# The second mixer of a two-layer trunk: the z tile between q and k, a weight residual behind the z scaling, turned output tiles in four PSUM banks, and the last two of them amid the early rows

## The chip, the cores and the metric

The kernel runs on one core of one Trainium2 chip. The metric is the device time of one execution in microseconds (us). Engines are named as in the profile: PE is TensorE (PEld its weight loads), DVE VectorE, ACT ScalarE, POOL GpSimd, SP the queue that issues most DMAs.

## The reference, cut to what matters

Two layers on 512 tokens of 1024 features, fp32. Layer 0 has a softmax mixer with forget gates and layer 1 a gated linear attention (GLA); each is followed by a squared-ReLU MLP of 4096. The change touches only the GLA mixer:

```python
def gla_mixer(h, w_in, w_gate_up, b_gate, g_norm, w_out):
    proj = h @ w_in                       # q 512, k 512, v 1024, z_lr 16, r 1024 columns
    q, k, v, z_lr, r = split(proj)
    g = log_sigmoid(z_lr @ w_gate_up + b_gate) / 16.0
    # 4 heads of 128 keys and 256 values, causal, decayed by exp(cumsum(g));
    # a state is carried from chunk to chunk
    o = o * rsqrt(mean(o * o) + EPS) * g_norm * silu(r)
    return o @ w_out
```

## The kernel before

**Precision.** Every fp32 weight unit (128 x 2048) and every activation is split into a high part that PE takes in its fast fp32r form (`w_hi`, `hT_hi`, made by ACT) and the residual (`w_lo`, `hT_lo`, made by DVE from the high part and the source). A product is three matmuls: lo·hi, hi·hi, hi·lo. `split_lo(0, 0, c)` makes the residual of weight unit c on DVE; `w_lo_made` counts the units in order. Four slots hold the units; SP loads unit c when `w_lo_made` says that unit c-4 is split.

**Order.** Each engine runs one instruction list that is written out by hand; semaphores carry the dependencies. An instruction that waits holds back all that stands behind it on its engine. There are eight PSUM banks of 128 x 512 fp32.

**Start of the GLA mixer.** PE projects q of head 0 (`project_gqk(0, 0)`, bank 0) and k of head 0 (`project_gqk(0, 1)`, bank 1), 24 matmuls of 512 columns each. Then four blocks against a matrix of ones put the norm's factor into bank 2 (L1492), which ACT copies out as `rstd_wide` (L871). Then comes the z tile (`gate_tile(3, 1)`, L1050 and L1054, 16 matmuls into bank 3). DVE scales it into `zT` (L1894) after the residuals of units GLA_U+1 to GLA_U+3 (`GR_U[0]` is GLA_U+3, the r weights of head 0). Then come the four gate tiles (L1498, two instructions each, banks 4 to 7). ACT and DVE turn these into the log-decays `gb`; v, r and the attention of head 0 follow.

**Attention of a head.** `level(a, lv)` is one of eight score products (L1424) into banks 0 and 1 in turn; DVE prepares its operands (`differences`, `decayed`) and merges its result (`keep`), ACT takes the exponentials (`decays`). `turn_tail(a)` transposes decayed keys through bank 2, `outer(a)` forms the state updates in banks 2 and 3, and `attend(a)` writes the outputs there (L1451, then L1455, which wait for the last `keep`). `project_gr(a, t)` projects r of head a, token block t, into banks 4 and 5; ACT's `tanhs` (L899) and DVE's `silus` (L1967, two instructions a head, counted by `silu_made`) turn it into silu(r).

**Turned output.** `turn_go(k)` transposes feature tile k of the mixer's output (four PE transposes, L1471). ACT's `keep_goT` (L910) makes its high part from that bank, and DVE's `keep_goT` (L1993) the residual, counted by `goT_lo_made`. Tiles 0 to 5 (heads 0 to 2) are turned amid the levels of head 3, by turns in banks 6 and 7. Tiles 6 and 7 need head 3's own output. The output projection starts early: `out_early(0, t)` takes feature tiles 0 to 3 and `out_early(1, t)` tiles 4 and 5 of token block t (L1034, L1037, L1038), and `add_rows` adds tiles 6 and 7, then the second half of the columns.

The two passages of PE's list that are reordered stand in the diff below. ACT's list near the second one is: `decays(3, 4)`, `tanhs(3, (0, 1))`, `decays(3, 5)`, `tanhs(3, (2, 3))`, `keep_goT(0)`, `keep_goT(1)`, `decays(3, 6)`, `keep_goT(2)`, `keep_goT(3)`, `turn_tail(3)`, `keep_goT(4)`, `keep_goT(5)`, `decays(3, 7)`. DVE's is: `keep(3, 2)`, `differences(3, 5)`, `decayed(3, 4)`, `silus(3)`, `differences(3, 6)`, `keep_goT(0)`, `keep_goT(1)`, `keep(3, 3)`, `decayed(3, 5)`, `keep_goT(2)`, `keep_goT(3)`, `keep(3, 4)` and on.

Of the kernel before, what the change touches and what calls it, by code (L numbers as in the profile page):

```python
# [17 lines left out]
TB = S // P  # L18
D = 1024
KT = D // P  # L20
# [6 lines left out]
GLA_H = 4  # L27
# [53 lines left out]
OUT_EARLY = 6  # L81
# [15 lines left out]


def goT_bank(k):
    return 6 + k % 2 if k < OUT_EARLY else k % 2  # L100


def turn_banks(head):
# [68 lines left out]
def fox_gla_trunk(nc, x, fox_w_in, fox_b_f, fox_w_out, gla_w_in, gla_w_gate_up, gla_b_gate,  # L172
# [12 lines left out]
    with ExitStack() as ctx:  # L185
# [829 lines left out]
        def _(pe):  # L1015
# [31 lines left out]
            def gate_tile(b, which, before):  # L1047

                def hi_and_lo(k):
                    return pe.matmul(bank[b][0:GATE_ROWS, :], gates_split[:, k, which * RANK:which * RANK + GATE_ROWS],  # L1050
                                     hT_hi[:, k, :], start=(k == 0), stop=(k == KT - 1))

                def hi_only(k):
                    pe.matmul(bank[b][0:RANK, :], gates_split[:, k, which * RANK:(which + 1) * RANK], hT_lo[:, k, :],  # L1054
                              start=False, stop=False)

                before(0)
                hi_and_lo(0)
                for k in range(1, KT):
                    before(k)  # L1060
                    hi_only(k - 1)
                    if k < KT - 1:
                        hi_and_lo(k)
                hi_only(KT - 1)
                a = hi_and_lo(KT - 1)
                return a
# [65 lines left out]
            def add_rows(i, per, c, x, ready_rows, early=False, between=None, done=0):  # L1132


                for half in range(2):
                    for kg in range(2):
                        j = 2 * half + kg
                        split_of(i, per, c + j)
                        if half == 0:
                            ready_rows(kg)  # L1140
                        for t in range(TB):
                            w, ks = unit(i, per, c + j), range(4 * kg, 4 * kg + 4)
                            if done and half == 0:
                                if kg == 0:
                                    continue
                                w, ks = [b[:, done - KT // 2:] for b in w], range(done, KT)
                            a = block_of_tokens(bank[sum_bank(half, t, early)][:], t, w, x, ks,
                                                kg == 0, kg == 1, t == 0)
                            if kg == 1:
                                a.then_inc(sum_done, 1)  # L1150
                        if between and j == 2:
                            between()
# [208 lines left out]
            def project_gqk(a, part, ks, before=None):  # L1361

                first = QK_BANK[0] if a == 0 else QK_BANK[1]
                w = [x[:, :, part * DK:(part + 1) * DK] for x in unit(0, 0, GQK_U[a], 2 * DK)]
                if (before or ks[0] == 0) and part == 0:
                    split_of(0, 0, GQK_U[a])
                    if a == 1:
                        pe.wait_ge(gv_copied, TB)
                    elif a:
                        pe.wait_ge(gk_copied, a)  # L1370
                to = bank[first + part][:]
                for k in ks:
                    if before:
                        before(k)
                    mm = pe.matmul(to, w[0][:, k, :], hT_lo[:, k, :], start=(k == (ks[0] if before else 0)), stop=False)  # L1375
                    if k == (ks[0] if before else 0) and part == 0:
                        mm.then_inc(w_begun, 1)
                    pe.matmul(to, w[0][:, k, :], hT_hi[:, k, :], start=False, stop=False)
                    mm = pe.matmul(to, w[1][:, k, :], hT_hi[:, k, :], start=False, stop=(k == (ks[-1] if before else KT - 1)))
                if before or ks[-1] == KT - 1:  # L1380
                    mm.then_inc((gq_done, gk_done)[part], 1)
# [18 lines left out]
            def project_gr(a, t):  # L1400

                if t == 0:
                    split_of(0, 0, GR_U[a])
                    pe.wait_ge(gv_copied, 2 if a < 2 else 2 * TB)
                    if a:
                        pe.wait_ge(silu_made, a * 2)
                mm = block_of_tokens(bank[4 + t // 2][:, (t % 2) * DV:(t % 2 + 1) * DV], t, unit(0, 0, GR_U[a], DV), hT,
                                     range(KT), True, True, t == 0)
                if t % 2:
                    mm.then_inc(r_done, 1)  # L1410

            def level(a, lv):

                if lv:
                    pe.wait_ge(ql_made, a * (2 * LEVELS) + 2 * lv)
                    qs, ks = ql[:, lv % 2, :], kl[:, lv % 2, :]
                else:
                    pe.wait_ge(gk_copied, a + 1)
                    pe.wait_ge(gq_copied, a + 1)
                    qs, ks = gq, gk  # L1420
                if a * (LEVELS + 1) + lv > 1:
                    pe.wait_ge(level_kept, a * (LEVELS + 1) + (lv - 1))
                for t in range(TB):
                    mm = pe.matmul(bank[LEVEL_BANK[lv % 2]][:, t * P:(t + 1) * P], ks[:, t * P:(t + 1) * P],  # L1424
                                   qs[:, t * P:(t + 1) * P], start=True, stop=True)
                mm.then_inc(level_done, 1)
# [33 lines left out]
            def turn_go(k):  # L1460
                if k < OUT_EARLY:
                    if k < 2:
                        pe.wait_ge(gk_copied, GLA_H)
                        pe.wait_ge(go_made, 3 * TB)
                    else:
                        pe.wait_ge(goT_lo_made, k - 1)
                else:
                    pe.wait_ge(go_made, GLA_H * TB)
                    pe.wait_ge(level_kept, GLA_H * (LEVELS + 1))
                for t in range(TB):  # L1470
                    mm = pe.transpose(bank[goT_bank(k)][:, t * P:(t + 1) * P], o_all[:, t, k * P:(k + 1) * P], ident[:])  # L1471
                mm.then_inc(go_turned, 1)
# [12 lines left out]

            lo, hi = range(KT // 2), range(KT // 2, KT)
            project_gqk(0, 0, ORDER[2], ready_late(2, GLA_ADDS))
            project_gqk(0, 1, range(KT))
            pe.wait_ge(gla_filled, 2)
            pe.wait_ge(only_made, 1)  # L1490
            for t in range(TB):
                mm = pe.matmul(bank[2][:, t * P:(t + 1) * P], root[:], only[:, t, :], start=True, stop=True)  # L1492
            mm.then_inc(wide_done, 1)
            gate_tile(3, 1, lambda k: None).then_inc(z_done, 1)
            pe.wait_ge(gup_loaded, 48)
            pe.wait_ge(z_scaled, 1)
            for a in range(GLA_H):
# [79 lines left out]
            level(3, 1)  # L1577
            project_gr(3, 2)
            level(3, 2)
            project_gr(3, 3)  # L1580
            turn_go(0)
            turn_go(1)
            level(3, 3)
            turn_go(2)
            turn_go(3)
# [10 lines left out]
            out_early(0, 2)  # L1596
            attend(3)
            out_early(0, 3)
            for t in range(TB):
                out_early(1, t)  # L1600
            turn_go(6)
            turn_go(7)
            add_rows(0, 0, GLA_OUT_U, hT, lambda kg: pe.wait_ge(goT_lo_made, 4 * kg + 4), False,
                     lambda: turn_left(3, MLP1_ADDS), OUT_EARLY)
            turn_right(3, MLP1_ADDS)
# [4 lines left out]
        def _(dve):  # L1610
            mine = Steps(dve, dve_step)

            def split_lo(i, per, c):

                slot = slot_of(c)
                dve.wait_ge(w_hi_made, i * per + (c + 1))
                dve.tensor_tensor(w_lo[:, slot, :], w_stage[:, slot, :], fp(w_hi[:, slot, :]),
                                  ALU.subtract).then_inc(w_lo_made, 1)
# [201 lines left out]
            def keep_qk(h):  # L1820
                dve.wait_ge(qk_hi_made, h + 1)
                dve.scalar_tensor_tensor(out=qk_lo[:], in0=bank[qk_bank(h)][:], scalar=qk_scale[:, 0:1], in1=fp(qk_hi[:]),
                                         op0=ALU.mult, op1=ALU.subtract).then_inc(qk_lo_made, 1)
# [62 lines left out]
            mlp(0, MLP0_U, MLP0_ADDS)  # L1886


            for unit in range(GLA_U + 1, GR_U[0] + 1):
                split_lo(0, 0, unit)  # L1890
            dve.wait_ge(z_done, 1)
            dve.wait_ge(gla_filled, 3)
# [18 lines left out]
            def gates(a):  # L1911

                dve.wait_ge(g_min, a + 1)
                dve.wait_ge(g_ln, min(a, 1) + 1)
                mine.then(dve.tensor_tensor(gb[:, a, :], gb[:, a, :], glog[:, a, :], ALU.subtract))
                dve.wait_ge(gla_filled, 4)
                dve.tensor_tensor_scan(gb[:, a, :], flat(restart[:]), gb[:, a, :], 0.0, ALU.mult, ALU.add).then_inc(gb_made, 1)
# [79 lines left out]
            for a in range(GLA_H):  # L1997
                dve.wait_ge(g_abs, a + 1)
                dve.tensor_scalar(gb[:, a, :], bank[4 + a][:], 0.0, None, ALU.min).then_inc(g_min, 1)
            keep_qk(0)  # L2000
            gates(0)
            differences(0, 1)
            tail_differences(0)
# [164 lines left out]
```

## Time and profile before

| what | value |
|---|---|
| time, median of 3 runs | 1178.92 us (1178.91, 1178.92 and 1181.81) |
| the profiled execution's own time | 1183.01 us |
| its span, first to last instruction | 1181.2 us |
| PE busy | 1157.6 us, 98% of the span |
| mean granted PE clock | 0.994 of full speed |
| GLA mixer, from q of head 0 to the last output sum | about 595 to 846 us |

A row of a timeline is a start in us, a duration in us, the engine and line, the operation with output and inputs and, behind x, how many instructions were merged. In brackets stands the engine's idle time before it and what ended it. A matmul's shown duration has its drain in it, so neighbouring matmuls overlap: the step from start to start is what one costs. A 512-column matmul steps by about 0.23 us, a 256-column one by 0.12 us, and a 128-column one or a transpose by 0.11 us.

### The profile page before, as it was taken

The numbers are of one execution on the slowest core, as the hardware profiler recorded it, in microseconds if no ns is written. First come the engines' busy times: TensorE is split into PE (matmuls) and PEld (weight loads), VectorE is DVE, ScalarE is ACT, GpSimd is POOL, SyncE is SP. The second block draws the span as 40 slices with busy tenths as digits, with TensorE's granted clock in tenths as the row PEclk, the third lists the DMA queues.
The fourth block names the chain that finished last, engine by engine and source line by source line (L and its number), as shares of the span: only waits on it lengthen the run. The fifth ranks groups of instructions, "written<-read, shape, count | busy, mean of one in ns | idle before, by whom it ended". The sixth has DMA issues, their size and how long they took to land.

```text
span 1181.2 us, 14703 instructions
## 1 busy us (share of the span) xinstructions
PE 1157.6 (98%) x5629; PEld 967.2 (82%) x5629; DVE 792.8 (67%) x986; ACT 558.9 (47%) x780; POOL 42.3 (4%) x90
## 2 busy tenths in 40 slices
PE   6999999999999999999999999999999999999997
PEld 5788888888888888888868998987888888888886
DVE  5537778635875856858856585493378578488487
ACT  6336666527434435435555332252455354363454
POOL 2000000000000000000020101010000000000001
PEclk9999999999999999999999999999999999999999
DMA  9248565432062161241540320204132513415202
GB/s 285 51 91 167 126 144 152 129 113 82 26 208 77 48 201 36 86 163 36 162 126 1 108 79 30 72 1 143 36 107 65 185 36 106 144 36 178 74 36 86
DMA packets 116136, 119.00 MB, mean 101 GB/s; under 512 B 38929, under 2 KB 84017, under 8 KB 116082
## 3 DMA queue, kind: packets, MB, share of 16 engines
q1 hardware_dynamic: 112992, 116.21, 32.9%
q10 hardware_dynamic: 3090, 2.05, 0.6%
q8 instruction: 36, 0.59, 0.2%
q14 instruction: 18, 0.15, 0.0%
HBM read 103.50 MB, written 2.10 MB: 89 GB/s over the span
## 4 chain that ended last, share of the span: by engine, by line
PE 95%; DVE 2%; ACT 1%; DMA 1%; issue 1%; POOL 0%; SPq 0%; POOLq 0%; ACTq 0%; DVEq 0%
PE bank L1025 10%; PE bank L1021 10%; PE bank L1024 10%; PE bank L1179 9%; PE bank L1184 8%; PE bank L1183 8%; PE bank L1034 6%; PE bank L1037 6%; PE bank L1038 6%; PE bank L1254 2%; PE bank L1258 2%; PE bank L1257 2%; PE bank L1424 2%; PE bank L1302 2%; PE bank L1289 1%; PE bank L1375 1%
## 5 line engine op out<-in xcount | busy, mean ns | idle before, releaser
L1626 DVE TENSOR_TENSOR w_lo<-w_stage,w_hi 128x2048 fp32r<-128x2048 f32 x88 | 200.5, 2286 | 33.4 <-ACT w_hi L628 11.9
L628 ACT ACTIVATE w_hi<-w_stage 128x2048 fp32r<-128x2048 f32 x80 | 152.0, 1912 | 148.9 <-PE bank L1179 92.4
L1021 PE MATMUL bank<-hT_lo,w_hi 128*128 128x512 f32 x512 | 199.8, 390 | 0.0
L1025 PE MATMUL bank<-hT_hi,w_lo 128*128 128x512 f32 x512 | 199.3, 389 | 0.0
L1024 PE MATMUL bank<-hT_hi,w_hi 128*128 128x512 f32 x512 | 199.2, 389 | 0.0
L1179 PE MATMUL bank<-w_lo,u_hi 128*128 128x512 f32 x336 | 131.7, 392 | 0.0
L1184 PE MATMUL bank<-w_hi,u_lo 128*128 128x512 f32 x336 | 130.8, 389 | 0.0
L1183 PE MATMUL bank<-w_hi,u_hi 128*128 128x512 f32 x336 | 130.8, 389 | 0.0
L1034 PE MATMUL bank<-w_lo,hT_hi 128*128 128x512 f32 (+1 forms) x320 | 116.5, 364 | 4.3 <-DVE hT_lo L1993 1.9
L1021 PEld LDWEIGHTS bank<-hT_lo,w_hi 128*128 128x128 f32 x512 | 96.1, 188 | 20.6 <-DVE hT_lo L1684 0.5
L1037 PE MATMUL bank<-w_hi,hT_hi 128*128 128x512 f32 (+1 forms) x320 | 112.4, 351 | 0.0
L1025 PEld LDWEIGHTS bank<-hT_hi,w_lo 128*128 128x128 f32 x512 | 96.1, 188 | 19.9
L1024 PEld LDWEIGHTS bank<-hT_hi,w_hi 128*128 128x128 f32 x512 | 96.1, 188 | 19.7
L1038 PE MATMUL bank<-w_hi,hT_lo 128*128 128x512 f32 (+1 forms) x320 | 112.3, 351 | 0.0
L1732 DVE SCALAR_TENSOR_TENSOR h<-bank,columns_of,h 128x512 f32<-128x512 f32 x112 | 80.6, 743 | 32.9 <-PE bank L1184 32.9
L715 ACT ACTIVATE u_raw<-bank 128x512 f32<-128x512 f32 x64 | 37.7, 590 | 90.2 <-PE bank L1025 90.0
L1179 PEld LDWEIGHTS bank<-w_lo,u_hi 128*128 128x128 f32 x336 | 63.1, 188 | 15.2 <-DVE h L1732 1.4
L1640 DVE TENSOR_TENSOR w_stage<-w_stage 128x2048 f32<-128x2048 f32 x32 | 73.2, 2286 | 1.2
L1184 PEld LDWEIGHTS bank<-w_hi,u_lo 128*128 128x128 f32 x336 | 63.1, 188 | 13.1
L1183 PEld LDWEIGHTS bank<-w_hi,u_hi 128*128 128x128 f32 x336 | 63.1, 188 | 12.9
L1034 PEld LDWEIGHTS bank<-w_lo,hT_hi 128*128 128x128 f32 x320 | 61.4, 192 | 13.5 <-issue 3.6
L1037 PEld LDWEIGHTS bank<-w_hi,hT_hi 128*128 128x128 f32 x320 | 61.6, 193 | 7.9 <-issue 0.5
(226 smaller groups left out, 1957.4 us busy)
## 6 DMA issues: line engine op xcount, KB each, us to landing
w_stage<-in_mlp_w_up_dram SPq DMA_DIRECT2D x32, 1024.0 KB, 5.6
w_stage<-in_mlp_w_down_dram SPq DMA_DIRECT2D x32, 1024.0 KB, 6.3
w_stage<-in_fox_w_in_dram SPq DMA_DIRECT2D x32, 256.0 KB, 4.7
w_stage<-in_gla_w_in_dram SPq DMA_DIRECT2D x8, 1024.0 KB, 5.3
w_stage<-in_fox_w_in_dram SPq DMA_DIRECT2D x4, 1024.0 KB, 8.7
qa<-qk_hi SPq DMA_DIRECT2D x32, 128.0 KB
w_stage<-in_fox_w_out_dram SPq DMA_DIRECT2D x4, 1024.0 KB, 5.4
w_stage<-in_gla_w_in_dram SPq DMA_DIRECT2D x8, 512.0 KB, 5.1
```

The costliest lines, as they stand in the source:

```text
L628: act.activation(w_hi[:, HI_SLOT[unit], :], w_stage[:, STAGE[unit], :], ACT.Copy).then_inc(w_hi_made, 1)
L1021: a = pe.matmul(out, w[0][:, k, :], x[1][:, k, :], start=(k == 0), stop=False)
L1024: pe.matmul(out, w[0][:, k, :], x[0][:, k, :], start=False, stop=False)
L1025: a = pe.matmul(out, w[1][:, k, :], x[0][:, k, :], start=False, stop=(k == KT - 1))
L1034: a = pe.matmul(out, xs[0], w[1][:, m, :], start=(first and m == 0), stop=False)
L1037: pe.matmul(out, xs[0], w[0][:, m, :], start=False, stop=False)
L1038: a = pe.matmul(out, xs[1], w[0][:, m, :], start=False, stop=(last and m == len(ks) - 1))
L1179: a = pe.matmul(out, xs[0], lo[:, k, :], start=(begins and k == 0), stop=False, skip_group_check=True)
L1183: pe.matmul(out, xs[0], hi[:, k, :], start=False, stop=False, skip_group_check=True)
L1184: a = pe.matmul(out, xs[1], hi[:, k, :], start=False, stop=(k == KT // 2 - 1), skip_group_check=True)
L1626: dve.tensor_tensor(w_lo[:, to, :], w_stage[:, at, :], fp(w_hi[:, to, :]), ALU.subtract).then_inc(w_lo_made, 1)
L1732: dve.scalar_tensor_tensor(out=to, in0=bank[PRODUCTS[n][2] + t][:], scalar=scale, in1=to, op0=ALU.mult, op1=ALU.add).then_inc(added, 1)
```

## The change

`gate_tile` moves from behind k and the ones product to the place between q and k of head 0, and the ones product goes between the two halves of k. On DVE the residual of unit GLA_U+3 moves from ahead of the scaling of z to behind the scaling of q and k of head 0. `goT_bank` puts tiles 2 and 3 in banks 4 and 5, so that the first four turned tiles have four banks; these two wait for the two `silus` of head 3, and tiles 4 and 5 now for tiles 0 and 1. `project_gr(3, 3)` moves behind `turn_go(0)` and `turn_go(1)`, and `turn_go(6)` and `turn_go(7)` move two rows forward in the second early pass. The arithmetic and the number of instructions stay as they were.

```diff
 def goT_bank(k):
-    return 6 + k % 2 if k < OUT_EARLY else k % 2
+    return 2 + k if k in (2, 3) else 6 + k % 2 if k < OUT_EARLY else k % 2
...
                     if k < 2:
                         pe.wait_ge(gk_copied, GLA_H)
                         pe.wait_ge(go_made, 3 * TB)
+                    elif k < 4:
+                        pe.wait_ge(silu_made, 2 * GLA_H + k - 3)
                     else:
-                        pe.wait_ge(goT_lo_made, k - 1)
+                        pe.wait_ge(goT_lo_made, k - 3)
...
             project_gqk(0, 0, ORDER[2], ready_late(2, GLA_ADDS))
-            project_gqk(0, 1, range(KT))
+            gate_tile(3, 1, lambda k: None).then_inc(z_done, 1)
+            project_gqk(0, 1, lo)
             pe.wait_ge(gla_filled, 2)
             pe.wait_ge(only_made, 1)
             for t in range(TB):
                 mm = pe.matmul(bank[2][:, t * P:(t + 1) * P], root[:], only[:, t, :], start=True, stop=True)
             mm.then_inc(wide_done, 1)
-            gate_tile(3, 1, lambda k: None).then_inc(z_done, 1)
+            project_gqk(0, 1, hi)
             pe.wait_ge(gup_loaded, 48)
             pe.wait_ge(z_scaled, 1)
...
             level(3, 1)
             project_gr(3, 2)
             level(3, 2)
-            project_gr(3, 3)
             turn_go(0)
             turn_go(1)
+            project_gr(3, 3)
             level(3, 3)
             turn_go(2)
             turn_go(3)
...
             attend(3)
             out_early(0, 3)
-            for t in range(TB):
+            for t in range(2):
                 out_early(1, t)
             turn_go(6)
             turn_go(7)
+            for t in range(2, TB):
+                out_early(1, t)
             add_rows(0, 0, GLA_OUT_U, hT, lambda kg: pe.wait_ge(goT_lo_made, 4 * kg + 4), False,
...
-            for unit in range(GLA_U + 1, GR_U[0] + 1):
+            for unit in range(GLA_U + 1, GR_U[0]):
                 split_lo(0, 0, unit)
             dve.wait_ge(z_done, 1)
...
             keep_qk(0)
+            split_lo(0, 0, GR_U[0])
             gates(0)
```

## Rows read from the trace of the kernel before

**Rows 1.** The page, its span and PE's busy time.
```profile
span 1181.2 us, 14703 instructions
PE 1157.6 (98%) x5629; PEld 967.2 (82%) x5629; DVE 792.8 (67%) x986; ACT 558.9 (47%) x780; POOL 42.3 (4%) x90
```
**Rows 2.** Waits of PE: who waited for whom, total us, times, longest us.
```profile
PE bank L1034 <- DVE hT_lo L1993: 1.9, 1, 1.9
...
PE bank L1471 <- DVE hT_lo L1993: 1.6, 1, 1.6
PE bank L1498 <- DVE zT L1894: 0.9, 1, 0.9
```
**Rows 3.** Windows of 5 us: busy of PE, PEld, DVE, ACT, POOL; PE clock; DMA.
```profile
615.00:620.00 5.00, 5.00 (x11) 2.88 (x10) 3.23 (x6) 3.16 (x5) 0.00 (x0) 0.50 0.61 214
620.00:625.00 5.00, 5.00 (x20) 4.05 (x19) 3.96 (x8) 4.93 (x6) 0.00 (x0) 0.83 0.00 0
...
780.00:785.00 5.00, 3.42 (x31) 3.23 (x30) 4.84 (x12) 3.14 (x6) 0.00 (x0) 1.00 0.00 0
...
815.00:820.00 5.00, 5.00 (x16) 3.92 (x17) 2.29 (x1) 0.68 (x1) 0.00 (x0) 0.66 0.15 29
820.00:825.00 5.00, 5.00 (x23) 4.12 (x22) 0.51 (x1) 1.92 (x1) 0.00 (x0) 1.00 1.03 363
```
**Rows 4.** Timeline of all engines around the z tile and the gate tiles.
```profile
607.05 1.05 PE L1492 MATMUL bank<-only,root 128*128 128x128 f32 x8
...
608.14 0.60 ACT L871 ACTIVATE o_all<-bank 128x512 f32<-128x512 f32 x1 [0.67 <-PE bank L1492]
...
609.11 2.28 DVE L1617 TENSOR_TENSOR w_lo<-w_stage,w_hi 128x2048 fp32r<-128x2048 f32 x1
...
611.83 0.68 DVE L1894 TENSOR_TENSOR zT<-bank,o_all 48x512 f32<-48x512 f32 x1 [0.45 <-PE bank L1050]
...
612.66 4.94 PE L1498 MATMUL bank<-zT,gup 65*128 65x512 f32 x8 [0.87 <-DVE zT L1894]
...
633.27 0.42 DVE L1935 TENSOR_TENSOR ql<-gq,decay 128x256 f32<-128x256 f32 x1 [8.45 <-ACT decay L890]
```
**Rows 5.** Timeline of PE, ACT and DVE, levels 2 to 5 of head 3.
```profile
777.52 1.06 PE L1424 MATMUL bank<-ql,kl 128*128 128x128 f32 x8
...
781.29 1.03 PE L1471 MATMUL bank<-ident,o_all 128*128 128x128 f32 x8
...
781.87 0.82 ACT L899 ACTIVATE gb<-bank,half_rstd 128x256 f32<-128x256 f32 x2
...
782.72 0.69 DVE L1967 SCALAR_TENSOR_TENSOR gb<-gb,bank 128x512 f32<-128x512 f32 x1 [0.16 <-ACT gb L899]
...
784.80 1.31 PE L1471 MATMUL bank<-ident,o_all 128*128 128x128 f32 x8 [1.58 <-DVE hT_lo L1993]
...
785.95 0.41 DVE L1935 TENSOR_TENSOR ql<-gq,decay 128x256 f32<-128x256 f32 x1
...
788.56 1.06 PE L1424 MATMUL bank<-ql,kl 128*128 128x128 f32 x8
```
**Rows 6.** Timeline, end of head 3's attention: its last merge, and PE at `attend`.
```profile
799.06 0.73 DVE L1950 COPY_PREDICATED o_all<-masks,bank 128x512 f32<-128x512 uint8 x1
...
800.76 1.46 PE L1451 MATMUL bank<-state,since 128*128 128x256 f32 x6
...
802.06 1.89 PE L1455 MATMUL bank<-gv,o_all 128*128 128x256 f32 x8
```
**Rows 7.** Timeline around the last two turned tiles.
```profile
806.50 0.88 DVE L1986 SCALAR_TENSOR_TENSOR o_all<-bank,orstd,gb 128x256 f32<-128x256 f32 x2 [0.25 <-POOL orstd L589]
...
811.98 1.03 PE L1471 MATMUL bank<-ident,o_all 128*128 128x128 f32 x8
...
813.33 1.41 DVE L1993 SCALAR_TENSOR_TENSOR hT_lo<-bank,gn,hT_hi 128x512 fp32r<-128x512 f32 x2 [5.95 <-ACT hT_hi L910]
...
814.89 0.47 PE L1034 MATMUL bank<-w_lo,hT_hi 128*128 128x512 f32 x1 [1.88 <-DVE hT_lo L1993]
```

## The prediction

> **What bounds the kernel.** I read the page first: PE is busy for 1157.6 of 1181.2 us [rows 1]. So a change can give only what PE loses by waiting or by a low clock; the other engines matter where they release it. The list of PE's waits comes next. Beside the start of the program it names three long ones, and all lie in the GLA mixer: 1.9 us for the residual of a turned output tile ahead of the last sums, 1.6 us for the same kind of residual at a turned tile amid head 3, and 0.9 us for `zT` [rows 2]. That is 4.4 us, or 0.37% of the span. Then I read the granted clock in windows, because a wait can cost more than itself. It was 1.00 nearly everywhere, but 0.50 and 0.83 in 615 to 625 us and 0.66 in 815 to 820 us [rows 3]. Each stretch begins some 2 us after one of these waits has ended. A window loses (1 - clock) times its length: 5 x 0.50 + 5 x 0.17 = 3.4 us behind the z wait and 5 x 0.34 = 1.7 us behind the last. The third wait lies in 780 to 785 us, where the clock stayed at 1.00 [rows 3]. No work is removed, so the sum below is one of waits, and of the clock behind them.
>
> **Part 1: z between q and k.** Now PE issues k (24 matmuls), the ones product, the z tile (16) and the gate tiles, which wait: the last z matmul ends at about 611.8, DVE scales for 0.68 us, and the gate tiles start at 612.66 [rows 4]. The trace puts 0.87 us down to that wait. Without it the gate tiles also need no drain of the z tile, another 0.15 us (611.8 is the end of a pipelined matmul; the next could have begun about one step of 5.00 / 22 = 0.23 us behind its start [rows 3]). Gain: 1.0 us.
>
> Does another wait take its place? With z first, 16 steps of 0.23 us, the ones product starts 3.6 us later for z and 12 x 0.23 = 2.7 us earlier for the half of k moved behind it: at 607.05 + 0.9 = 608.0 [rows 4]. It takes 1.05, ACT's copy 0.60, so `rstd_wide` is there at 609.7. DVE has been free since about 609.1, since the residual of 2.28 us that stood there [rows 4] is gone. `zT` is ready at 609.7 + 0.1 + 0.68 = 610.5, and PE gets to the gate tiles only at 611.6. The slack is 1.1 us. Had the residual stayed, DVE would have been free at 611.4 and `zT` ready at 612.1, a wait of half a microsecond: that is what the DVE edit is worth, not more.
>
> The moved residual (2.28 us) now stands ahead of `gates(0)`. I take it at nothing, because DVE later sat idle for 8.45 us until 633.27 for ACT's exponential, itself held by v's evacuations [rows 4]. Without that cover it would cost up to 2.3 us. SP's load of unit GLA_U+7 goes out when that residual is done, some 11 us later; its consumer on ACT comes at the start of head 1, tens of microseconds later, so it too is hidden. The range keeps 0 to 2.3 us for both.
>
> **Part 2: four banks, and r behind the first turned tiles.** Before, PE starts level 2 at 777.52, r's last block, two turned tiles at 781.29, level 3, and then waits 1.58 us until 784.80 for a free bank. Level 5 starts at 788.56 [rows 5]. Of the 3.76 us between, 27 steps of 0.11 us (16 for tiles 2 to 5, 3 for the tail, 8 for level 4) are 3.0; the other 0.8 are short hand-overs from bank to bank. After, tiles 0 and 1 start at 778.4 and end at 779.2 and r's block (24 steps of 0.12 us) at 782.1. Tile 2 needs the first `silus`, which is done at 782.6; level 3 ends at 782.9, so there is no wait. Tile 3 needs the second. Its chain is r's block, ACT's two tanhs (0.82 us) and DVE's 0.69 us [rows 5]: 782.2 + 0.85 + 0.7 = 783.8. PE is ready at 783.4, a new wait of 0.4 to 0.5 us. The tanhs start 0.4 us later than now (781.87), so DVE, busy without a gap here, runs 0.4 us late: the operands of level 5, now made from 785.95 on, are ready at about 787.1. PE has done tiles 4 and 5 by 786.4 and waits a second time, 0.7 us. Level 5 starts at 787.1 to 787.3 instead of 788.56. Gain: 1.2 us. What is late next is DVE's last merge: now it ends at 799.8 and `attend` starts at 800.76, with the matmuls that need the merge at 802.06 [rows 6]. With DVE 0.4 late it ends at 800.2, and PE would want it at 802.06 - 1.2 = 800.8. Slack 0.6 us, so the gain passes. Bounds: 0 (DVE hands the delay on) and 2.3 (all hand-overs gone).
>
> **Part 3: tiles 6 and 7 between the early rows.** Before, they are turned at 811.98 and PE waits for their residuals until 814.89, 1.88 us by the trace and 2.0 with the drain [rows 7]. After, two early blocks of 6 x 0.23 = 1.4 us each stand behind the 0.9 us of transposes, 3.6 us in all, against a chain (start of turning to the second residual) of 814.74 - 811.98 = 2.8 us [rows 7]. The wait is covered with 0.8 us to spare. The data are there: head 3's output is done at 807.4 and the tiles would be turned from 809.3 on, both by the present clock [rows 7]. Gain: 2.0 us, and I see no way to lose it; bounds 1.5 and 2.1.
>
> **The clock.** The 1.7 us behind the last wait go with it, if the wait drew the fall; the stretch before has only dense 512-column work. The 3.4 us behind the z wait are less sure. The clock fell while the gate tiles ran, which use 65 rows of the array [rows 4], and those stay. I take half, 1.7 us, with bounds 0 and 3.4.
>
> **The sum.** From the profiled execution's own 1183.0: 1.0 + 1.2 + 2.0 = 4.2 of waits and 1.7 + 1.7 of clock, to 1175.4. The median of the runs, though, is 1178.9, 4.1 below that execution, and two of the three runs agree within 0.01 us while the third is 2.9 above. Such steps have the size of the clock losses, so I take it that the median has few of them. Waits alone give 1178.9 - 4.2 = 1174.7; all the clock on top gives 1169.6. I forecast 1174.4, a little clock gained. 0.3% (3.5 us) is about what a measurement of this kernel can tell from no change, so "faster" means under 1175.4.
>
> **Rivals.**
> *The turned tiles draw a clock fall.* With two waits (0.5 and 0.7 us) among 19 transposes, PE's clock may fall between 783 and 788. Against it: the same stretch had 1.58 us idle and the same transposes at clock 1.00 [rows 3]. For it: a wait of 1.88 us behind transposes was followed by a fall. One fall like that costs 1.7 us: 1176.1. By the Trainium skill (TensorE: Matmul & The Clock Gate, Part 4: PE-mode transpose), transposes do not count as busy PE as matmuls do. By that rule the stretch would fall; the trace does not agree for 780 to 785, where the clock held.
> *The second part gives nothing.* DVE is the bound between levels 3 and 7; its delay of 0.4 us meets slacks of 0.6. If `silus` come 1 us later than I reckon, part 2's gain is gone: 1175.7.
> *All clock comes back.* If the timed runs had the falls too, and dense work around the gate tiles prevents them: 1169.6 to 1172, taken as 1171.
> *Slower than before.* One mechanism: `turn_go(3)` now stands before `turn_tail(3)` and level 4 and waits for ACT's tanhs and DVE's `silus`, each behind other work. A stall of s there costs s - 0.5, plus 1.7 for a clock fall like that of the last wait; from 3.0 us on it eats all 4.2. A stall of 4 us gives 1174.4 + 3.5 + 1.7 = 1179.6. Against it: my order of the chain puts `silus` at 783.8 with nothing longer than 0.85 us ahead.
>
> **Chances.** Forecast 0.62 (its own range 1173 to 1176; one tenth of it above 1175.4); clock fall 0.13; part 2 nothing 0.12; all clock back 0.08; slower 0.05. Faster by over 0.3%: 0.54 + 0.08 and a little of the middle cases' lower edge, 0.64. Slower by over 0.3%: 0.03. The rest, 0.33, is within 0.3%. The range leaves out half of the last clock case and the slower one: 1171.0 to 1177.5, the upper end being waits alone with 2.8 us given back (part 2 and one fall).
>
> **What would show it.** The profile after should have no wait of L1498 for `zT` and none of L1034 for the residual of L1993; a wait of some 0.5 us of L1471 for `silus` (L1967), one of 0.7 us of L1424 for DVE's operands; a clock of 1.00 at the last sums; DVE idle still some 5 us ahead of the first `decayed`. The forecast is wrong if the timed runs had other clock losses than the profiled one, or if the gate tiles draw a fall by themselves in every run.

## The result, and the profile after

The changed kernel takes 1174.35 us (median of 5 runs, 1174.21 to 1174.66); the kernel before, on the same chip, takes 1178.92 us (median of 5, 1178.81 to 1181.89). By the medians that is 4.6 us, or 0.4%, faster. The ratio over the runs is 0.9949 with a 95% interval of 0.9936 to 0.9963; two of the five runs of the kernel before lie some 3 us above the other three. The profiled execution took 1174.36 us with a span of 1172.6.

The page after, its span and busy times, to be held against [rows 1]:
```profile
span 1172.6 us, 14703 instructions
PE 1152.5 (98%) x5629; PEld 964.9 (82%) x5629; DVE 793.1 (68%) x986; ACT 558.7 (48%) x780; POOL 42.2 (4%) x90
```
The number of instructions is the same and the busy times of DVE, ACT and POOL moved by 0.3 us at most. PE's fell by 5.1 us. No matmul was removed, so that is in the main matmuls that ran slow before. The waits of PE after (who waited for whom, total us, times, longest us):
```profile
PE bank L1214 <- DMA gain_rows<-in_norm_mlp_g_dram: 9.0, 1, 9.0
PE bank L1034 <- DVE hT_lo L1681: 1.6, 2, 0.8
...
PE bank L1424 <- DVE kl L1942: 0.5, 1, 0.5
...
PE bank L1473 <- DVE gb L1972: 0.4, 1, 0.4
```
The three waits of [rows 2] are gone. L1214 is the start of the program and L1681 the other mixer; both are as before. New are two short ones in head 3: `turn_go` (L1473, before L1471) waits for `silus` (L1972, before L1967), and `level` (L1424) waits for its operand `kl`. The windows after (busy time of PE, PEld, DVE, ACT, POOL, PE's granted clock, DMA share, GB/s):
```profile
615.00:620.00 5.00, 5.00 (x21) 3.77 (x21) 4.66 (x6) 4.64 (x6) 0.00 (x0) 1.00 0.15 37
620.00:625.00 5.00, 5.00 (x24) 4.13 (x23) 4.32 (x8) 4.96 (x5) 0.00 (x0) 1.00 0.62 203
780.00:785.00 5.00, 4.17 (x33) 3.90 (x34) 5.00 (x13) 3.99 (x8) 0.00 (x0) 1.00 0.00 0
785.00:790.00 5.00, 5.00 (x28) 4.28 (x26) 4.90 (x13) 3.83 (x3) 0.00 (x0) 1.00 0.01 3
815.00:820.00 5.00, 5.00 (x23) 4.13 (x22) 4.12 (x5) 2.04 (x5) 0.00 (x0) 1.00 0.70 236
```
The clock is 1.00 where [rows 3] had 0.50, 0.83 and 0.66. PE's busy time of 5.00 in 615 to 620 is the same in both; what differs is that 21 matmuls were done in it and not 11.

**The measuring stick.** The whole change lies between q's projection and the end. So from here on I measure from the first matmul of L1375, which is q's, to the end of the span. All matmuls of L1375 in the kernel before (shortest, median and longest ns, first start and last end):
```profile
L1375 PE MATMUL bank<-hT_lo,w_hi x64: 389/389/578, 595.4 to 749.0; 128*128 128x512 f32 x64
```
and after:
```profile
L1375 PE MATMUL bank<-hT_lo,w_hi x64: 389/389/578, 596.0 to 745.3; 128*128 128x512 f32 x64
```
Before, 1181.2 - 595.4 = 585.8 us; after, 1172.6 - 596.0 = 576.6 us. The difference is 9.2, and 0.6 us of it is lost again ahead of q, where the two kernels are the same. The clock accounts for 3.4 + 1.7 = 5.1 of the 9.2. What is left is 580.7 against 576.6, the waits: 4.1 to 4.2 with the rounding.

**The z tile.** Timeline of all engines after, to be held against [rows 4]:
```profile
608.62 1.05 PE L1495 MATMUL bank<-only,root 128*128 128x128 f32 x8
609.71 0.60 ACT L871 ACTIVATE o_all<-bank 128x512 f32<-128x512 f32 x1 [1.68 <-PE bank L1495]
610.43 0.68 DVE L1899 TENSOR_TENSOR zT<-bank,o_all 48x512 f32<-48x512 f32 x1 [0.69 <-ACT o_all L871]
612.24 3.60 PE L1501 MATMUL bank<-zT,gup 65*128 65x512 f32 x8
618.31 2.28 DVE L1622 TENSOR_TENSOR w_lo<-w_stage,w_hi 128x2048 fp32r<-128x2048 f32 x1
629.51 0.43 DVE L1940 TENSOR_TENSOR ql<-gq,decay 128x256 f32<-128x256 f32 x1 [5.12 <-ACT decay L890]
```
`zT` is ready at 611.11, and PE comes to the gate tiles at 612.24 without a wait: 1.1 us to spare. Their eight matmuls take 3.60 us against 4.94. The moved residual (618.31) is followed by an idle time of 5.12 us of DVE, so it cost nothing.

**Head 3.** Timeline of PE, ACT and DVE after, to be held against [rows 5, 6]:
```profile
773.76 1.05 PE L1424 MATMUL bank<-ql,kl 128*128 128x128 f32 x8
774.65 1.04 PE L1473 MATMUL bank<-ident,o_all 128*128 128x128 f32 x8
...
778.68 0.84 ACT L899 ACTIVATE gb<-bank,half_rstd 128x256 f32<-128x256 f32 x2 [0.47 <-PE bank L1038]
779.55 0.69 DVE L1972 SCALAR_TENSOR_TENSOR gb<-gb,bank 128x512 f32<-128x512 f32 x1 [0.73 <-ACT gb L899]
780.29 0.65 PE L1473 MATMUL bank<-ident,o_all 128*128 128x128 f32 x4 [0.40 <-DVE gb L1972]
...
783.11 0.42 DVE L1942 TENSOR_TENSOR kl<-gk,decay 128x256 f32<-128x256 f32 x1
783.58 1.16 PE L1424 MATMUL bank<-ql,kl 128*128 128x128 f32 x8 [0.54 <-DVE kl L1942]
...
795.89 0.73 DVE L1955 COPY_PREDICATED o_all<-masks,bank 128x512 f32<-128x512 uint8 x1
795.90 1.46 PE L1451 MATMUL bank<-state,since 128*128 128x256 f32 x6
797.19 1.89 PE L1455 MATMUL bank<-gv,o_all 128*128 128x256 f32 x8
```
Level 2 starts 3.76 us earlier than before (777.52 - 773.76) and level 5 4.98 us earlier (788.56 - 783.58): the second part gave 1.22 us. `attend` starts 4.86 us earlier (800.76 - 795.90). The missing 0.1 us is lost at level 5 itself, whose eight matmuls take 1.16 us behind their wait where they took 1.06. DVE's last merge costs nothing: it ends at 796.62 and the matmuls that need it (L1455) start at 797.19 without a wait.

**The last two turned tiles.** Timeline after, to be held against [rows 7]:
```profile
804.39 1.04 PE L1473 MATMUL bank<-ident,o_all 128*128 128x128 f32 x8
...
805.75 1.41 DVE L1998 SCALAR_TENSOR_TENSOR hT_lo<-bank,gn,hT_hi 128x512 fp32r<-128x512 f32 x2 [3.24 <-ACT hT_hi L910]
...
808.00 0.39 PE L1034 MATMUL bank<-w_lo,hT_hi 128*128 128x512 f32 x1
```
The residuals are done at 807.16, and the sums that need them begin at 808.00 with no wait: 0.8 us to spare.

### The profile page after: what moved, and what is told of

Same layout as the page of the kernel before. It is cut to its first block, busy times and chain, and to the rows that moved or that the text cites. A ratio compares the mean times of both kernels' runs of the same rounds, so it can differ in the third digit from the quotient of the medians.

```text
span 1172.6 us, 14703 instructions
## 1 busy us (share of the span) xinstructions
PE 1152.5 (98%) x5629; PEld 964.9 (82%) x5629; DVE 793.1 (68%) x986; ACT 558.7 (48%) x780; POOL 42.2 (4%) x90
## 4 chain that ended last, share of the span: by engine, by line
PE 97%; DMA 1%; ACT 1%; DVE 1%; issue 0%; SPq 0%; POOL 0%; POOLq 0%; ACTq 0%; DVEq 0%
PE bank L1021 10%; PE bank L1024 10%; PE bank L1025 10%; PE bank L1179 9%; PE bank L1183 9%; PE bank L1184 9%; PE bank L1034 6%; PE bank L1038 6%; PE bank L1037 6%; PE bank L1254 2%; PE bank L1258 2%; PE bank L1257 2%; PE bank L1424 2%; PE bank L1302 2%; PE bank L1289 1%; PE bank L1375 1%
## 5 line engine op out<-in xcount | busy, mean ns | idle before, releaser
L1179 PEld LDWEIGHTS bank<-w_lo,u_hi 128*128 128x128 f32 x336 | 63.1, 188 | 15.3 <-DVE h L1737 1.4
L1718 DVE TENSOR_TENSOR u_raw<-u_raw 128x256 f32<-128x256 f32 x32 | 13.5, 422 | 80.5 <-ACT u_raw L717 80.5
```

What stands on the lines that cost most here:

```text
L1179: a = pe.matmul(out, xs[0], lo[:, k, :], start=(begins and k == 0), stop=False, skip_group_check=True)
```

## The experiments

My theory has two halves. First, the waits: the three parts are worth 1.0, 1.2 and 2.0 us, each whatever becomes of the other two. Second, the clock: its falls come only behind those waits, so they go with them, though not every execution has them. The main rival for the clock is that the gate tiles, which use 65 rows of the array, draw the fall at z by themselves. For the waits the rivals are that a part gives nothing (its gain is handed on to another engine) or that the new waits cost more than they replace.

**1. The kernel before, again (before_again).** No edit.

> The kernel before, unchanged, timed as if it were a change, so that each run's span and granted clock are listed. Theory A (the two levels of its times, 1178.9 and 1181.8 us, are clock falls that some runs have and some have not): the runs at about 1181.8 show a lower mean clock than those at 1178.9, by 2.9 / 1180 x 2 = about 0.005. Theory B (the levels come from elsewhere, transfers or the launch): the mean clock is the same in both. Ratio 1.000 by either.

Measured: 1179.07 us median (1178.56 to 1181.66, 11 runs) beside 1179.1 (1178.33 to 1181.69, 27 runs), ratio 0.9996 [0.9988, 1.0005]. Times gather at 1178.3 to 1179.8 and some 3 us higher: 2 of these 11 runs and 5 of the 27 lie above 1181. The profiled execution was one of the high ones, 1181.66 us. Its windows:
```profile
615.00:620.00 5.00, 5.00 (x10) 2.85 (x9) 3.40 (x6) 3.33 (x5) 0.00 (x0) 0.53 0.66 227
620.00:625.00 5.00, 5.00 (x19) 3.97 (x18) 4.03 (x8) 4.94 (x5) 0.00 (x0) 0.79 0.00 0
...
815.00:820.00 5.00, 4.84 (x21) 4.05 (x22) 2.31 (x2) 0.95 (x1) 0.00 (x0) 1.00 0.08 18
```
The same program and the same waits, but only the z fall (5 x 0.47 + 5 x 0.21 = 3.4 us), and none at the last sums. The profile of [rows 3] had both and was slower than any run timed in this case. I had wanted to sort the runs by a difference of some 0.005 in their mean granted clock. It wasn't there: both groups show 0.997. My figure was too large, since a loss of 3.4 us where another run loses 1.7 us moves the mean by 1.7 / 1180 = 0.0014. And the mean also counts the half clock that is granted from 2.5 to 5 us behind PE's last matmul to the end of the span, which in the profiles stands for 0.7 to 1.9 us of such a loss and costs no time. So windows are needed to tell those two falls apart. The mean does tell of no fall at all: three of the 38 runs (1178.33, 1178.56 and 1178.64 us) show 1.000, which leaves no room for a loss of 1.7 us.

**2. Each part alone, on the kernel before (only_z, only_turned, only_late).**
```diff
 # only_z, on PE, and split_lo(0, 0, GR_U[0]) behind keep_qk(0) on DVE
-            project_gqk(0, 1, range(KT))
+            gate_tile(3, 1, lambda k: None).then_inc(z_done, 1)
+            project_gqk(0, 1, lo)
...
-            gate_tile(3, 1, lambda k: None).then_inc(z_done, 1)
+            project_gqk(0, 1, hi)
```
```diff
 # only_turned; goT_bank and the waits of turn_go as in the change
-            project_gr(3, 3)
             turn_go(0)
             turn_go(1)
+            project_gr(3, 3)
```
```diff
 # only_late
-            for t in range(TB):
+            for t in range(2):
                 out_early(1, t)
             turn_go(6)
             turn_go(7)
+            for t in range(2, TB):
+                out_early(1, t)
```

> The kernel before with part 1 alone: the z tile between q and k, the residual behind the scaling of q and k. Waits alone: 1.0 us off the median, 1177.9. In the profile no wait of the gate tiles for zT and clock 1.00 in 610 to 625 us; the wait of 1.9 us at the last sums stays, with its clock fall where the run has one. Rival (the gate tiles draw the fall by themselves): the clock still falls in 612 to 622 us although the wait is gone.

> The kernel before with part 2 alone: tiles 2 and 3 in banks 4 and 5, r's last block behind the first two turned tiles. Waits alone: 1.1 to 1.2 us off the median, 1177.8. In the profile the wait of 1.6 us at tile 2 is replaced by 0.4 us for silus and 0.5 us for level 5's operands. Rival (DVE hands the delay on to its last merge): level 5 starts 1.2 us earlier but attend does not, and the median stays at 1178.9.

> The kernel before with part 3 alone: tiles 6 and 7 turned behind two of the four early rows. Waits alone: 2.0 us off the median, 1176.9; with the clock fall behind it up to 3.7. In the profile no wait of the last sums for the residuals, and clock 1.00 around 815 us. Rival (the gain of the whole change is mostly part 3 and its clock): 1175.3, and the two other parts alone give almost nothing.

Measured, with the clock's losses read from the windows. Two more profiles of the kernel before, told under 4, stand beside them.

| kernel | median us (runs) | ratio [95%] | q to end | clock lost | q to end without it |
|---|---|---|---|---|---|
| before, as first profiled | 1178.92 (5) | | 585.8 | 3.4 + 1.7 | 580.7 |
| before_again | 1179.07 (11) | 0.9996 [0.9988, 1.0005] | 584.2 | 3.4 | 580.8 |
| before_look2, before_look3 | | | 582.5, 582.4 | 1.7, 1.7 | 580.8, 580.7 |
| only_z | 1176.97 (9) | 0.9977 [0.9967, 0.9987] | 579.8 | 0 | 579.8 |
| only_turned | 1177.03 (12) | 0.9984 [0.9974, 0.9994] | 579.7 | 0 | 579.7 |
| only_late | 1176.47 (5) | 0.9967 [0.9954, 0.998] | 578.7 | 0 | 578.7 |
| after | 1174.35 (5) | 0.9949 [0.9936, 0.9963] | 576.6 | 0 | 576.6 |

The last column settles the first half of the theory. Four profiles of the kernel before agree on 580.7 to 580.8 once the clock's losses are taken off. Against 580.8 the parts give 1.0, 1.1 and 2.1 us, and together 4.2: the sum of the three, with nothing lost between them.

The timed medians don't add up so. They fell by 2.1, 2.1 and 2.6 us against 1179.1, where by waits alone I expected 1.0, 1.1 to 1.2 and 2.0. Together that is 6.8 us, where the whole change gave 4.6. An estimate from each run's own span shows why. The span less the last column is the moment at which q started, if the run lost nothing to the clock; in the profiles q started at 594.8 to 596.1. The nine runs of only_z, the nine lower ones of only_turned and the five of only_late give 594.6 to 596.1, so by this estimate they lost nothing. The lower group of the kernel before gives 595.8 to 597.2, so most of its runs lost something, as the two at the median did (1.7 us, see 4). This loss thus went with each part alone. It is counted three times in the 6.8 us, and it went in only_z and only_turned although the wait of 1.9 us ahead of the last sums stayed.

The second half of the theory, the clock, holds only in part. Waits in only_z:
```profile
PE bank L1034 <- DVE hT_lo L1994: 1.9, 1, 1.9
```
It kept the wait ahead of the last sums. Its clock held all the same: the window 810 to 815 of only_z, in which that wait ends,
```profile
810.00:815.00 5.00, 3.87 (x17) 3.26 (x18) 3.28 (x3) 1.92 (x2) 0.00 (x0) 1.00 0.02 3
```
and the windows behind it are at 1.00. The window behind the z wait in only_late, which kept its 0.9 us for `zT` as only_turned did:
```profile
615.00:620.00 5.00, 5.00 (x20) 3.47 (x19) 3.92 (x6) 4.22 (x6) 0.00 (x0) 1.00 0.74 246
```
So a fall can follow a wait and need not, one that was frequent can be gone when its wait comes a microsecond earlier, and nothing shows the gate tiles drawing it by themselves: they run in every kernel here, and none of the eight profiles without the 0.9 us wait fell at them. In the timed runs, only_turned shows the 3 us step too, 3 of its 12 runs lying at 1180.0 to 1180.5, with a mean granted clock of 0.996 where the other nine have 0.998 or 0.999. Taken over all runs of this case, 15 of the 72 of kernels with the z wait lie some 3 us above the rest, and none of the 36 of kernels in which it is gone or shortened to 0.3 us. That ties the step to the z wait in the timed runs too.

**3. The changed kernel again, and three kernels with its new waits changed (after_again, banks_only, silu_split, packed).** after_again has no edit. banks_only puts r's last block back ahead of the first turned tiles and keeps the four banks. silu_split lets DVE make level 6's differences between the two halves of `silus(3)`. packed adds to silu_split that PE turns tile 3 behind level 4 and tile 5 behind level 5.
```diff
 # banks_only, on the changed kernel
+            project_gr(3, 3)
             turn_go(0)
             turn_go(1)
-            project_gr(3, 3)
```
```diff
 # silu_split, on the changed kernel; silus gets the halves it is to do
-            silus(3)
+            silus(3, (0,))
             differences(3, 6)
+            silus(3, (1,))
```
```diff
 # packed: silu_split and this on PE; on DVE keep_goT(1) moves behind decayed(3, 5)
             turn_go(2)
-            turn_go(3)
             turn_tail(3)
             level(3, 4)
+            turn_go(3)
             turn_go(4)
-            turn_go(5)
             level(3, 5)
+            turn_go(5)
```

> The changed kernel, unchanged, beside the three variants below on one chip, as their reference. 1174.4 us; ratio to before 0.995 to 0.997. Theory (its runs differ only by when the clock first rises at the start, since no wait is left that draws a fall in the mixer): spread under 1.5 us and no run at +3 us. Rival (falls come whatever the waits): some runs at 1177.

> The changed kernel with r's last block back ahead of the first two turned tiles, the four banks kept. Theory (DVE's chain from the second silus to level 5's operands is the bound there, and moving r's block only made it late by 0.4 to 0.5 us): level 5 starts 0.5 us earlier than in the changed kernel, the wait for silus is gone, 0.5 us off its time. Rival (the moved block covers the wait for the residuals): a wait of more than a microsecond at turned tiles, slower than the changed kernel by 0.5 us or more.

> The changed kernel with DVE's level-6 differences of head 3 put between the two silus, into the 0.73 us in which DVE waits for the tanhs. Theory (DVE's chain is the bound up to level 5): level 5's operands are ready 0.6 to 0.7 us earlier, PE's wait of 0.54 us there disappears or shrinks to 0.1, 0.5 to 0.7 us off. Rival (PE's own list is the bound there): the time stays that of the changed kernel.

> As the one with the differences between the silus, and besides: PE turns tile 3 behind level 4 and tile 5 behind level 5, and DVE makes tile 1's residual behind level 5's operands. Theory: both waits (0.40 and 0.54 us) go, 0.9 to 1.0 us off the changed kernel. Rival (DVE's last merge becomes the bound at attend, where it has 0.5 us of slack): about 0.6 us off, with a wait of the last output matmuls for the merge instead.

Measured on one chip, beside the kernel before at 1179.55 us (1178.87 to 1182.67, 9 runs):

| kernel | median us (lowest to highest) | ratio [95%] | q to end |
|---|---|---|---|
| after_again | 1173.79 (1173.03 to 1174.41) | 0.9949 [0.9936, 0.9963] | 576.6 |
| banks_only | 1173.47 (1173.33 to 1173.7) | 0.9948 [0.9935, 0.9962] | 576.0 |
| silu_split | 1173.13 (1172.81 to 1173.5) | 0.9946 [0.9932, 0.9959] | 575.9 |
| packed | 1173.24 (1171.89 to 1173.45) | 0.9943 [0.9929, 0.9957] | 575.7 |

Each of the three has one of the new waits less. Timeline of banks_only, DVE's second `silus` and level 5:
```profile
778.57 0.69 DVE L1972 SCALAR_TENSOR_TENSOR gb<-gb,bank 128x512 f32<-128x512 f32 x1 [0.16 <-ACT gb L899]
...
782.61 1.16 PE L1424 MATMUL bank<-ql,kl 128*128 128x128 f32 x8 [0.54 <-DVE kl L1942]
```
Compare with the changed kernel, where the same `silus` came at 779.55 after DVE had been idle for 0.73 us. With r's block first, DVE idles for 0.16 only and PE never waits for it at a turned tile. Level 5 starts 187.0 us behind q's first matmul, against 187.6, and the q-to-end time is 0.6 us shorter, as expected. So the four banks bring the second part's gain and more (banks and order were parted on top of the other two parts, not on the kernel before); moving r's block behind the first two turned tiles costs 0.6. In silu_split, level 5 has no wait:
```profile
778.97 0.69 DVE L1972 SCALAR_TENSOR_TENSOR gb<-gb,bank 128x512 f32<-128x512 f32 x1
...
782.33 1.16 PE L1424 MATMUL bank<-ql,kl 128*128 128x128 f32 x8
```
DVE used its idle time for the differences. What is left there is the 0.4 us for `silus`. In packed the wait for `silus` is gone and level 5 waits for 0.3:
```profile
782.27 1.16 PE L1424 MATMUL bank<-ql,kl 128*128 128x128 f32 x8 [0.27 <-DVE kl L1942]
```
By q to end, packed is the shortest at 575.7, 0.9 us under the changed kernel, and silu_split gives 0.7 of that; both as expected. In the timed runs these two are 0.55 to 0.66 us below after_again by their medians, but the intervals of all four ratios overlap widely; the gain over the changed kernel is read from the traces, and the timed runs alone wouldn't show it. banks_only with the split `silus` would combine the two edits; it wasn't tried.

**4. The slack of the first and third part, and the kernel before twice more (residual_stays, three_rows, before_look2, before_look3).** residual_stays leaves the weight residual ahead of the scaling of z, and three_rows puts three and one early rows around the last two turned tiles instead of two and two. before_look2 and before_look3 have no edit; they were to show an execution near the median of the kernel before.
```diff
 # residual_stays, on the changed kernel
-            for unit in range(GLA_U + 1, GR_U[0]):
+            for unit in range(GLA_U + 1, GR_U[0] + 1):
                 split_lo(0, 0, unit)
...
-            split_lo(0, 0, GR_U[0])
```
```diff
 # three_rows, on the changed kernel
-            for t in range(2):
+            for t in range(3):
                 out_early(1, t)
             turn_go(6)
             turn_go(7)
-            for t in range(2, TB):
+            for t in range(3, TB):
```

> The kernel before once more, one look. Most of its runs end near 1179 us and some at 1181.5. Theory (the three waits cost the same in every run, and what differs is whether and where the clock falls): a run near 1179 shows the same waits of 1.9, 1.6 and 0.9 us, and at most one fall of some 3.4 us at the lower level, costing 1.7 us or less. Rival: a run near 1179 has shorter waits than the profiled one of 1183.

> The changed kernel with the residual of unit GLA_U+3 back ahead of the scaling of z on DVE. Theory: DVE is free only at about 611.9 instead of 609.7, zT is ready at 612.6 and the gate tiles wait about 0.5 us; from q's first matmul to the end 0.5 us more than the changed kernel's 576.6 us. Rival 1: the wait is hidden all the same, 576.6. Rival 2: even half a microsecond of wait draws the clock fall of the kernel before, 3.4 us more, 580.

> The changed kernel with tiles 6 and 7 turned behind three of the four early rows, so that only one stands between them and their use. Theory: the chain from the start of turning to the second residual takes 2.8 us and is covered by 0.9 + 1.4 us, so a wait of 0.4 to 0.5 us appears at the last sums; 577.1 us from q's first matmul to the end, and no clock fall. Rival: the chain is shorter than 2.3 us and nothing changes.

> A third look at the kernel before, for the same question as the second: near 1179 us I expect the waits unchanged and one fall at most; at 1181.5 one fall of 6.8 us behind the z wait; at 1183 both falls.

Measured: one time each, 1179.04 us for before_look2, 1179.08 for before_look3, 1173.84 for residual_stays and 1174.1 for three_rows; the kernel before beside them took 1181.1. q to end is 577.0 for residual_stays and 577.2 for three_rows (577.1 was expected of both), 0.4 and 0.6 us more than the changed kernel. Timeline of residual_stays, around z:
```profile
606.57 4.48 DVE L1622 TENSOR_TENSOR w_lo<-w_stage,w_hi 128x2048 fp32r<-128x2048 f32 x2
610.97 0.68 DVE L1899 TENSOR_TENSOR zT<-bank,o_all 48x512 f32<-48x512 f32 x1
611.79 1.53 PE L1501 MATMUL bank<-zT,gup 65*128 65x512 f32 x3 [0.29 <-DVE zT L1899]
```
The residual in front makes `zT` late enough for a wait of 0.29 us. With the drain of the matmuls before it, the gate tiles start 0.45 us later than in the changed kernel, counted from q (611.79 - 595.1 against 612.24 - 596.0). Timeline of three_rows, at the last sums:
```profile
806.15 1.41 DVE L1998 SCALAR_TENSOR_TENSOR hT_lo<-bank,gn,hT_hi 128x512 fp32r<-128x512 f32 x2 [4.59 <-ACT hT_hi L910]
807.71 0.47 PE L1034 MATMUL bank<-w_lo,hT_hi 128*128 128x512 f32 x1 [0.50 <-DVE hT_lo L1998]
```
With one early row instead of two behind the tiles, 0.8 us to spare becomes a wait of 0.50. The clock was at 1.00 in both.

The windows of before_look2:
```profile
615.00:620.00 5.00, 5.00 (x22) 3.87 (x21) 3.83 (x7) 4.66 (x6) 0.00 (x0) 1.00 0.47 174
...
810.00:815.00 5.00, 3.98 (x11) 3.14 (x12) 3.16 (x3) 1.80 (x2) 0.00 (x0) 0.66 0.02 3
```
Here the z wait (0.9 us) drew nothing and the wait of 1.9 us ahead of the last sums cost 1.7 us of clock; before_look3 shows the same. Both executions are at the median of the kernel before. The first matmul of L1375 in before_look2:
```profile
L1375 PE MATMUL bank<-hT_lo,w_hi x64: 389/389/578, 594.8 to 745.2; 128*128 128x512 f32 x64
```
This is 1.2 us earlier than in the changed kernel's profile.

## Why the prediction was right, and which of its terms were not

**Part 1 was right.** 1.0 us forecast, 1.0 measured (only_z). The slack of 1.1 us for `zT` came out at 1.1. Had the residual stayed, I reckoned with half a microsecond; the gate tiles came 0.45 us later, 0.29 of it shown as a wait, and the time to the end grew by 0.4. I took the moved residual at nothing, and DVE idled for 5.12 us behind it.

**Part 2 was right as a whole.** 1.2 forecast, 1.22 between level 2 and level 5, 1.1 alone to the end. Both new waits came where they were put: 0.40 for `silus` (forecast 0.4 to 0.5) and 0.54 for level 5's operand (0.7). DVE ran 0.6 us late from `silus` on and not 0.4 (779.55 + 3.76 = 783.3 against 782.72), and the slack of 0.6 us at the last merge was still there: 0.57 (797.19 - 796.62). What I didn't ask is which of its two edits earns the gain. The banks do; the order of r's block takes 0.6 us of it back by making ACT's tanhs, and so DVE, late.

**Part 3 was right.** 2.0 forecast, 2.1 alone. The 0.8 us to spare were there, and one row less behind the tiles turned them into a wait of 0.50 (three_rows).

**The clock: two terms were mis-sized, in opposite directions.** The sum against the profiled execution gave 1183.0 - 4.2 - 3.4 = 1175.4, where 1174.4 was measured. I kept half of the z fall, 1.7 us, for the gate tiles' narrow work. All of it went: 1183.0 - 4.2 - 5.1 = 1173.7, and 0.6 us of a later start of q brings it to 1174.3. The step that failed is "I take half".

The other is "I take it that the median has few of them". Two executions at the median (1179.04 and 1179.08) had the 1.7 us fall at the last sums, which the forecast reckoned at nearly nothing. From there the reckoning is 1179.0 - 4.2 - 1.7 = 1173.1, plus the 1.2 us by which q started later in the changed kernel's profile, 1174.3. So the forecast of 1174.4, waits alone and a little clock, met the time partly because a clock loss that I thought the median hadn't got was nearly made up by a later start that I didn't foresee. That part was luck. The waits, 4.2 of the 4.6 us, are shown. The three runs of the kernel before with a mean granted clock of 1.000 say the same without any profile: they took 1178.5 us, and 1178.5 - 4.2 = 1174.3. That the earlier part is 594.8 us in some executions and 596.0 in others isn't the change's doing: the kernel before alone gave 594.8 to 595.7. A later first rise of the clock at the start of the program went with a later q in the 14 profiles, by and large (12.9 us and 594.8 in before_look2, 15.3 us and 596.0 in the changed kernel). The rise can be seen in PE's first work, the 32 transposes of L1081: they start 0.21 us apart before it and 0.11 us after it.

**Small slips.** Three sums of the prediction are off by a little, and none moves the forecast: one tenth of 0.62 leaves 0.56 below 1175.4 and not 0.54; part 2 and one fall are 2.9 us and not 2.8; and the last of the two stretches of low clock began 1.4 us behind its wait, not some 2.

**The rivals.** That the turned tiles draw a fall did not happen: the clock was 1.00 in 780 to 790 us in every profile, with all the transposes and waits of 0.40 and 0.54 us among them. The rule of the Trainium skill that spoke for it (TensorE: Matmul & The Clock Gate, Part 4: PE-mode transpose) made me reckon with a fall here, and the trace doesn't agree. Nor does it at the start of the program, where the clock rose to full in the midst of the 32 transposes, with one other transpose and no other work of PE ahead of them. That part 2 gives nothing is refuted by only_turned. "All clock comes back" happened in the traces, at 5.1 us, but the timed median had only 1.7 of it to give, so it didn't reach 1171. The stall of `turn_go(3)` was 0.40 us, below the 0.5 from which I counted it a loss.

**What stays open.** Why the same wait of 0.9 or 1.9 us is followed by a fall in one execution and not in the next. In four profiles of the kernel before, the two in which the clock first rose at 12.9 and 13.1 us fell only at the last sums, and the two at 14.2 and 14.6 us at z (one of them at both). The three kernels with one part each kept one or both of those waits, had their first rise at 15.4 to 16.0 us, and fell nowhere. That hints that the moment of the first rise matters, but it is a pattern in seven profiles and no experiment, and it can't be all: the 18 runs of only_z and only_turned that lost nothing had, by the estimate from their spans, q start over the whole range of 594.6 to 596.1 us. It also means that one profile without a fall proves little of a kernel: the changed kernel's own two rose at 15.3 and 15.4 us. What speaks for the change are three_rows, residual_stays, silu_split and banks_only, which rose at 13.4, 13.7, 14.0 and 14.5 us, in the range in which the kernel before fell (12.9 to 14.6), and stayed at 1.00. Likewise the steps of 3 us between timed runs have the size of the z fall, and the profiled executions at 1181.66 and 1183.01 us had it while those at 1179.0 hadn't; for the other timed runs there is only the mean granted clock, and it is 0.994 for the one at 1182.67 us, as for the profile with both falls. None of the 10 timed runs of the changed kernel and none of the 15 of its three variants lay 3 us above the rest.

## What to carry to other kernels

Where one engine is busy for 98% of the span, list its waits by length and read the granted clock behind each: in this kernel 4.4 us of waits had up to 5.1 us of clock behind them. Don't credit a part with its timed median alone: by the estimate above, each of the three here also took a clock loss of 1.7 us with it that could go only once. Cover such a wait by a block that is already there, reckon the slack on both sides of the move from rows, and name the next wait; here every slack came out within 0.3 us. When a part holds two edits, cost them apart: the free banks earned the gain here, and the reordering beside them lost a third of it again (0.6 of 1.8 us).

## What was unexpected of the hardware

Waits as short as 0.87 and 1.88 us were followed, 0.6 to 2.4 us after their end, by a granted clock of half speed (1.2 GHz in place of 2.4) that cost 3.4 and 1.7 us, up to four times the wait. The same waits went without a fall in other executions: the z wait of 0.9 us was followed by one in 2 of 6 profiles that had it, and the wait of 1.9 us ahead of the last sums in 3 of 6. The wait of 1.6 us amid head 3 was followed by none in the 6 profiles that had it. At the start of the program the clock rose to full while PE did nothing but transposes. And 1.2 us of the spread between executions arose ahead of q, in a part that no kernel here changed.
